# Weights of the last and the third pair from the end in column halves, other tile order and later residual reads at the end of a fused transformer and mixture-of-experts layer

## What is computed

```
x  = x + g1 * (concat([attn, rec]) @ w_out)          # "x1" below, the residual
h2 = modulate(rms_norm(x), sh2, sc2)
# top-1 of 4 groups, then top-2 of 8 experts inside it, weights in combine[n, e]
hg, hu = h2 @ w_gate[e], h2 @ w_up[e]                # 1024 -> 256
act    = silu(hg) * hu * combine[:, e]
y      = sum over e of act @ w_down[e]               # 256 -> 1024
out    = x + g2 * y
```

## Time and profile before

| what | us |
|---|---|
| median of 3 runs | 633.35 |
| the three runs | 629.74, 634.2, 633.35 |
| the profiled execution's own time | 631.55 |
| its span in the trace | 629.6 |

### The profile page before, as it was taken

How to read it: one execution, slowest core, us unless ns; L and a number is a source line. 1 busy time by engine, 2 the same in 40 slices (tenths; PEclk the granted TensorE clock), 3 DMA queues, 4 the chain that set the end, 5 groups by cost and what they waited for, 6 DMA issues and landing times.

```text
span 629.6 us, 9459 instructions
## 1 busy us (share of the span) xinstructions
PE 593.3 (94%) x3309; PEld 331.4 (53%) x3310; DVE 352.3 (56%) x788; ACT 177.5 (28%) x369; POOL 94.6 (15%) x131
## 2 busy tenths in 40 slices
PE   4989999999998999999999889999999999689797
PEld 2544555555565676645555445555555555355453
DVE  2736898765664888655666873343424334313337
ACT  4203887601144787731111101101110110011110
POOL 4000011122161000000000111212122121201200
PEclk9999999999999999999999999999999999989999
DMA  8999843330029629529114959999999999999876
GB/s 318 375 370 361 318 156 138 140 133 2 0 83 280 249 92 264 238 102 398 67 68 161 382 188 392 417 419 416 420 420 410 420 417 421 419 421 416 360 280 263
DMA packets 48273, 176.23 MB, mean 280 GB/s; under 512 B 10988, under 2 KB 18168, under 8 KB 34544
## 3 DMA queue, kind: packets, MB, share of 16 engines
q1 hardware_dynamic: 36992, 154.86, 63.0%
q0 software_dynamic: 6688, 15.58, 7.1%
q10 hardware_dynamic: 4560, 5.35, 2.4%
HBM read 163.31 MB, written 21.14 MB: 293 GB/s over the span
## 4 chain that ended last, share of the span: by engine, by line
PE 67%; DMA 15%; SPq 7%; DVE 6%; issue 2%; ACT 1%; ACTq 1%; POOL 1%; DVEq 0%; POOLq 0%
PE ps L1757 16%; PE ps L1574 11%; PE ps L1773 7%; PE ps L1490 7%; PE ps L1502 6%; DMA expert_w<-exp_w_up 5%; PE ps L1612 4%; PE ps L1639 4%; DMA gate_w<-lru_wx 3%; PE ps L1621 3%; DMA w_mod_ring<-w_mod 2%; SPq L329 2%; SPq L358 2%; PE ps L1465 2%; PE ps L1725 2%
## 5 line engine op out<-in xcount | busy, mean ns | idle before, releaser
L1757 PE MATMUL ps<-expert_w,hT_mixT 128*64 128x256 f32 x1120 | 137.1, 395 | 11.9 <-DMA expert_w<-exp_w_up 11.6
L1757 PEld LDWEIGHTS ps<-expert_w,hT_mixT 128*64 128x64 f32 x1120 | 84.8, 137 | 67.6 <-issue 23.0
L1490 PE MATMUL ps<-hT_mixT,w 128*128 128x128 f32 (+1 forms) x256 | 72.6, 437 | 1.2 <-DVE hT_mixT L918 1.2
L1574 PE MATMUL ps<-w,hT_mixT 128*128 128x512 f32 x160 | 71.9, 597 | 0.0
L1773 PE MATMUL ps<-expert_w,w 128*64 128x512 f32 x280 | 65.8, 598 | 0.0
L741 ACT ACTIVATE w<-ps 128x128 f32<-128x128 f32 x36 | 10.0, 278 | 194.4 <-PE ps L1757 194.4
L1304 DVE SCALAR_TENSOR_TENSOR w<-w,ps 128x128 f32<-128x128 f32 x36 | 10.4, 288 | 88.0 <-ACT w L741 88.0
L1490 PEld LDWEIGHTS ps<-hT_mixT,w 128*128 128x128 f32 x256 | 38.9, 191 | 35.8 <-issue 32.6
L1502 PE MATMUL ps<-w_qkv,hT_mixT 128*128 128x512 f32 (+1 forms) x160 | 53.2, 488 | 0.2 <-DVE v_tok L1006 0.2
L1322 DVE TENSOR_TENSOR w<-ps,w 128x1024 f32<-128x1024 f32 x17 | 20.8, 1225 | 56.5 <-PE ps L1773 56.5
L1574 PEld LDWEIGHTS ps<-w,hT_mixT 128*128 128x128 f32 x160 | 29.1, 191 | 29.9 <-issue 29.7
(11 more groups left out here) (289 smaller groups left out, 763.6 us busy)
## 6 DMA issues: line engine op xcount, KB each, us to landing
expert_w<-exp_w_down SPq DMA_DIRECT2D x31, 1024.0 KB, 18.5
expert_w<-exp_w_gate SPq DMA_DIRECT2D x29, 1024.0 KB
expert_w<-exp_w_up SPq DMA_DIRECT2D x29, 1024.0 KB
w_mod_ring<-w_mod SPq DMA_DIRECT2D x14, 1024.0 KB, 6.5
y_rows<-zero_rows POOLq DMA_DIRECT2D x10, 512.0 KB, 9.4
expert_w<-y_rows SPq DMA_DIRECT2D x10, 512.0 KB, 8.3
recurrence<-w_mod SPq DMA_DIRECT2D x8, 512.0 KB, 9.7
w<-w_in SPq DMA_DIRECT2D x4, 1024.0 KB, 16.9
```

The costliest lines, as they stand in the source:

```text
L1490: ins = pe.matmul(ps[:, bank, 0:n], w1v[:, c, m * P:(m + 1) * P], HM[:, c, lo:lo + n], start=(c == 0), stop=(c == DC - 1))
L1574: ins = pe.matmul(ps[:, 2 * (t % 2) + half, :], HM[:, c, t * P:(t + 1) * P], w1v[:, c, half * 512:(half + 1) * 512], start=(c == 0), stop= ...
L1757: ins = pe.matmul(ps[r, 2 + k, 0:2 * P].rearrange("p (k f) -> p k f", k=2), xT[:, c, r], gate_up(i)[:, :, c, k:FF:FC], start=(c == 0), sto ...
```

## The change

In `refill_for_halves` SP issues gate and up of pair 13 and of pair 15 as column halves: the four first halves, counted on a semaphore of their own (`lead_in` for pair 13, `halves_in` for pair 15), and then the four second halves, counted on `wgu_in[s]`. PE waits for the first halves ahead of the first half of its gate/up matmuls and for the second halves ahead of the second. The bytes are the same, and down is loaded as before. The x1b reads move behind the y_rows reads of the first two tiles, so behind the wait for the last scatter. The tiles at the end are worked in the order 3, 4, 0, 1, 2. Tiles 3 and 4 need no x1b, and no longer wait for it. PE_SUMS becomes 4, 0, 1. DVE does `with_second(3)` ahead of the last y's eviction.

```diff
-PE_SUMS = (1, 2, 3)
+ORDER = (3, 4, 0, 1, 2)
+PE_SUMS = (4, 0, 1)
...
+            def refill_for_halves(q, s, leading):
+
+                done = sp.value_load(last[0:1, q - HELD:q - HELD + 1])
+                sp.wait_ge(S["gu_mm"], done * FC)
+                for half in range(2):
+                    for j in range(2 * s, 2 * s + 2):
+                        for src, lo in ((wg_v, 0), (wu_v, EW)):
+                            sp.dma_start(ring[:, HOME[j], lo + half * EW // 2:lo + (half + 1) * EW // 2],
+                                         src[q * 2 + (j - 2 * s), :, half * EW // 2:(half + 1) * EW // 2])\
+                              .then_inc(wgu_in[s] if half else leading, 16)
+                sp.wait_ge(S["dn_mm"], done)
+                for j in range(2 * s, 2 * s + 2):
+                    w_down(sp, q * 2 + (j - 2 * s), j)
...
-            refill(PAIRS - 3, 1)
+            refill_for_halves(PAIRS - 3, 1, lead_in)
             refill(PAIRS - 2, 2, both=1)
             sp.dma_start(iota, ...)
-            refill(PAIRS - 1, 0)
-            sp.wait_ge(kept_in, 16 * 4)
-            for t in range(SPILLED):
-                sp.dma_start(x1b[:, t, :], a["x1_rows"][t * P:(t + 1) * P, :]).then_inc(kept_in, 16)
+            refill_for_halves(PAIRS - 1, 0, halves_in)
...
-            for t in range(NT):
+            sp.wait_ge(kept_in, 16 * 4)
+            for t in ORDER:
                 sp.dma_start(yk[:, t, :], ...).then_inc(rows_in[t], 16)
                 sp.dma_start(y0[:, t, :], ...).then_inc(y0_in[t], 16)
+                if t == ORDER[1]:
+                    for k in range(SPILLED):
+                        sp.dma_start(x1b[:, k, :], a["x1_rows"][k * P:(k + 1) * P, :]).then_inc(kept_in, 16)
...
             def with_second(t):
 
                 dve.wait_ge(rows_in[t], 32)
-                dve.wait_ge(kept_in, 16 * (4 + SPILLED))
+                if t < SPILLED:
+                    dve.wait_ge(kept_in, 16 * (4 + SPILLED))
...
+            with_second(3)
             last_y_evict(end)
+            with_first(3)
+            finish(0)
+            with_second(4)
             with_second(0)
-            with_first(0)
+            finish(1)
             with_second(1)
-            finish(0)
+            finish(2)
             with_second(2)
-            finish(1)
-            with_second(3)
-            with_second(4)
-            finish(2)
-            with_first(4)
+            with_first(2)
             finish(3)
             finish_last()
...
-                else:
+                elif not by_halves:
                     pe.wait_ge(wgu_in[s], visit * 64)
-                if s == 0 and not (isinstance(visit, int) and visit == 1):
+                if by_halves == 1:
+                    pe.wait_ge(lead_in, 64)
+                elif by_halves == 2:
+                    pe.wait_ge(halves_in, 128)
+                elif s == 0 and not (isinstance(visit, int) and visit == 1):
                     pe.wait_ge(halves_in, 64)
                 for half in range(2):
+                    if by_halves and half:
+                        pe.wait_ge(wgu_in[s], visit * 64)
```

More of the change, by code:

```diff
@@ L245, in build @@
         h2_at = [sem(f"h2_at{i}") for i in range(2)]
-        x1_at, last_rows, kept_in, halves_in = (sem(n) for n in ("x1_at", "last_rows", "kept_in", "halves_in"))
+        x1_at, last_rows, kept_in, halves_in, lead_in = (sem(n) for n in ("x1_at", "last_rows", "kept_in", "halves_in", "lead_in"))
         wm_in = [sem(f"wm_in{i}") for i in range(6)]
@@ L499, in _ @@
             sp.sem_inc(S["sp_turn"], 1)
-            for t in range(NT):
+            sp.wait_ge(kept_in, 16 * 4)
+            for t in ORDER:
                 sp.dma_start(yk[:, t, :], a["y_rows"][TOK + t * P:TOK + (t + 1) * P, :]).then_inc(rows_in[t], 16)
                 sp.dma_start(y0[:, t, :], a["y_rows"][t * P:(t + 1) * P, :]).then_inc(y0_in[t], 16)
-            for t in range(NT - 1):
-                sp.wait_ge(S["fin"], t + 1)
-                sp.dma_start(y_dst[t], yk[:, t, :]).then_inc(S["out_done"], 16)
+                if t == ORDER[1]:
+                    for k in range(SPILLED):
+                        sp.dma_start(x1b[:, k, :], a["x1_rows"][k * P:(k + 1) * P, :]).then_inc(kept_in, 16)
+            for i in range(NT - 1):
+                sp.wait_ge(S["fin"], i + 1)
+                sp.dma_start(y_dst[ORDER[i]], yk[:, ORDER[i], :]).then_inc(S["out_done"], 16)
             for half in range(2):
@@ L508, in _ @@
                 cols = slice(half * 512, (half + 1) * 512)
[L509 removed]
+                sp.dma_start(y_dst[ORDER[-1]][:, cols], yk[:, ORDER[-1], cols]).then_inc(S["out_done"], 16)
             sp.wait_ge(S["out_done"], 16 * (NT + 2))
@@ L1343, in with_first, with finish @@
                 step(dve.tensor_tensor(yk[:, t, :], yk[:, t, :], y0[:, t, :], ALU.add))
-            def finish(t):
-                dve.wait_ge(S["tail_mm"], t + 1)
-                b = 2 * t % 8
+            def finish(i):
+                dve.wait_ge(S["tail_mm"], i + 1)
+                t, b = ORDER[i], 2 * i % 8
                 dve.tensor_tensor(yk[:, t, :], yk[:, t, :], wide[:, b * 512:b * 512 + D], ALU.add)\
@@ L1351, in finish_last @@
             def finish_last():
-                b = 2 * (NT - 1) % 8
+                t, b = ORDER[-1], 2 * (NT - 1) % 8
                 for half in range(2):
@@ L1356, in finish_last @@
                     cols = slice(half * 512, (half + 1) * 512)
-                    dve.tensor_tensor(yk[:, NT - 1, cols], yk[:, NT - 1, cols], ps[:, b + half, :], ALU.add)\
+                    dve.tensor_tensor(yk[:, t, cols], yk[:, t, cols], ps[:, b + half, :], ALU.add)\
                        .then_inc(S["fin"], 1)
@@ L1730, in act_in, with step_of @@
                 pe.transpose(ps[:, 4 + 3 * c, 0:P], act2[:, c, :], ident[:, :]).then_inc(S["aT_mm"], 1)
-            def step_of(n, s, visit, kept=False):
+            def step_of(n, s, visit, kept=False, by_halves=0):
                 def gate_up(i):
@@ L1788, in _, with visits @@
             pe.wait_ge(S["route_ok"], 3)
-            def visits(q, s, visit, kept=False):
+            def visits(q, s, visit, kept=False, by_halves=0):
                 lo = pe.value_load(first[0:1, bass.ds(q, 1)])
@@ L1793, in visits @@
                 with pe.Fori(lo, hi) as n:
-                    step_of(n, s, visit, kept)
+                    step_of(n, s, visit, kept, by_halves)
             for s in range(HELD):
@@ L1800, in _ @@
             for q in range((BODIES - 1) * HELD, PAIRS):
-                visits(q, q % HELD, 1 + q // HELD, kept=q == KEPT // 2)
+                visits(q, q % HELD, 1 + q // HELD, kept=q == KEPT // 2, by_halves={PAIRS - 3: 1, PAIRS - 1: 2}.get(q, 0))
             steps = pe.value_load(last[0:1, PAIRS - 1:PAIRS])
@@ L1806, in _ @@
             pe.wait_ge(S["xT_a"], steps + 1)
-            for t in range(NT):
-                if t >= 4:
-                    pe.wait_ge(S["fin"], t - 3)
+            for i, t in enumerate(ORDER):
+                if i >= 4:
+                    pe.wait_ge(S["fin"], i - 3)
                 if t in PE_SUMS:
@@ L1812, in _ @@
                 for half in range(2):
-                    if t == 0:
+                    if i == 0:
                         pe.wait_ge(S["y_v"], steps + 1 + half)
                     if t in PE_SUMS:
-                        pe.matmul(ps[:, 2 * t % 8 + half, :], ident[:, :], y0[:, t, half * 512:(half + 1) * 512],
+                        pe.matmul(ps[:, 2 * i % 8 + half, :], ident[:, :], y0[:, t, half * 512:(half + 1) * 512],
                                   start=True, stop=False)
-                    ins = pe.matmul(ps[:, 2 * t % 8 + half, :], chosen[:, t, :],
+                    ins = pe.matmul(ps[:, 2 * i % 8 + half, :], chosen[:, t, :],
                                     y[:, half * 512:(half + 1) * 512], start=t not in PE_SUMS, stop=True)
-                    if half or t == NT - 1:
+                    if half or i == NT - 1:
                         ins.then_inc(S["tail_mm"], 1)
```

## The result

The change is slower, not faster: 634.34 us in the median of 20 runs against 632.32 for 20 runs of before, ratio 1.0036 with a 95% interval of 1.0023 to 1.0049, so 1.5 to 3.1 us and some 2.3. It lies inside my range and on the wrong side of no change. My rival 1 had this side and about this size (0.8 to 2.2 us), but not this path.

A forecast was written before the change was run, and what follows sets the result against it. It took the weight stream to bound late expert steps, and scatter plus reads the end. Pair 13's 0, pair 15's 4.8 us off the last path, and + 0.8 - 2.0 gave -1.2; it named 631.2 us, range 627.0 to 635.0.

The forecast's parts named there:

- rival 1: Tail bound by reads: x1b ahead of 603 delayed nobody; +0.8 us, with dear DMAs +2.2; chance 0.27.
- Pair 13: Its halves remove PE's 1.77 us wait, but PE then waits for pair 14's gate/up; gain taken as 0.
- Pair 15: Its halves let gate/up start at 593.0 without the 3.3 us wait; last step's path 4.8 us shorter.
- DVE's list: Tile 3's residual add moves into DVE's idle time before the eviction; 14.6 us behind it instead of 15.8.
- The reads: Tail reads start from 603.09 as before; three x1b reads among them make the last of 13 land at 623.4.
- + 0.8 - 2.0: Reads' path at the end: 0.8 us later by added x1b reads, 2.0 us earlier by x1b leaving the stream.
- Its path: The end hangs on the last of 13 reads, then 3.7 us of DVE and 3.3 us: 630.4.
- The pace: Tail reads land one after another at intervals of 1.34 us per 0.5 MB.
- The relief: x1b out of the stream ahead of 603 speeds the scatter and first reads; 0 to 3.8 us, taken as 2.0.
- -1.2: Predicted net change of the span, on the path through the tail's reads that ends last: 1.2 us faster.
- SP's queue: Eight more DMAs may hold SP longer, but its idle time from 580.5 to 603.09 covers it; no cost.
- Small DMAs: Halved weight DMAs cost 0.3 us, counted in the 2.0; by the fixed-cost rule some 14 us worse, thought unlikely.

The follow-up runs named there:

- dummies: The change with 12 dummy matmuls ahead of pair 14's step, filling PE's idle time there; ratio 1.0038 to before.
- pair 13 whole: The change with pair 13's weights loaded whole again instead of in halves; ratio 1.0036 to before.
- tail-alone trace: The change with all weights loaded whole as before, keeping its tile order and late x1b reads; ratio 1.0021 to before.
- the runs with dummies: The change with added dummy matmuls: 12 ahead of pair 14 (1.0038), or 6 (1.0053) or 3 (1.0027) where PE waits for tile 0's y0.
- 3 dummies: The change with 3 dummy matmuls of 512 columns where PE waits for tile 0's y0; ratio 1.0027 to before.
- early x1b: The change with the three x1b reads back in front of the wait for the last scatter; ratio 0.9989 to before.
- the run with all edits together: The change with pair 13 whole, x1b reads early, eviction before tile 3's add, and PE's matmuls needing no y0 first; ratio 0.9981 to before.

## Why the prediction was wrong, point by point

- **Pair 13: right.** 0 us, since pair 14's weights are late next. The new wait there was 1.2 to 2.4 us in the traces where I had 1.7, and both runs on it show no effect within their 0.2%. That the clock can fall in this wait I had not said; with dummies in it the time was the same.
- **Pair 15: right on its path.** 593.0 and 7.42 us, 0.3 us of waiting for down. By the steps' own measure 4.7 of the 4.8 us were there.
- **DVE's list: half right.** The add ahead of the eviction isn't hidden: it waits for tile 3's rows and holds the eviction back by 1.6 us in the trace with pair 13 whole (PE waits 0.2 to 3.1 us for the eviction in the other traces with pair 15 in halves and the add in front).
- **The reads: this is the step that failed**, the term "+ 0.8 - 2.0" of the sum, in three parts.
  - *Its path.* I let the end hang on the last of 13 reads and 3.7 us of DVE. The longer path starts at the ninth, tile 0's y0: 607.3 + 8 x 1.34 = 618.0 by my own numbers, then 3.4 us of PE, 6.1 us of five DVE operations and 3.3 us, 630.8 instead of 630.4.
  - *The pace.* In the tail-alone trace SP's first read went out at 602.5 and landed 3.7 us later, at 606.2, and tile 0's y0 landed at 618.8. That makes eight intervals of 1.58 us, not 1.34, 1.9 us more; 5.5 us of them lie between the landing of the first x1b read (612.0) and that of the next y_rows read (617.5), three intervals. Why these were slower no run shows. PE's sum took 3.7 us, 0.3 more.
  - *The relief.* I took 2.0 us for x1b leaving the stream, and the first read landed at 606.2 instead of 607.3, so 1.1 us.

  So 0.8 + 0.4 + 1.9 + 0.3 - 1.1 = 2.3 us where I had -1.2, and the tail-alone trace has 631.9 against 629.6. This account is of one traced execution; the timed runs of the tail alone put the loss at 1.3 us (0.3 to 2.3).

  Nor is the relief one number. With x1b late the scatters issued at 595.4 to 596.4 took 6.8 to 7.1 us to land, against 7.58 and 7.78 with x1b early; but the one issued at 597.6 took 5.3, against 7.3 for those issued at 597.2 with x1b early. There my 2.0 us came, and they are in the change's own trace too (599.48, 4.97 us). The path and the pace are what that could not pay for.
- **What I left out: PE's idle time turns into a lower clock where its work lies on the path.** Pair 15's halves bring PE to the tail 5 us sooner and x1b keeps tile 0's y0 away, so it idles 2.7 to 4.2 us in three traces, and the sum of tile 0 takes 5.4 us instead of 3.7. This fits with the tail alone (1.0021, idle 1.88 us, sum 3.7) being no slower than the change (1.0036), although its last step ends 4.6 us later than with pair 15 in halves and pair 13 whole (610.4 against 605.8). But the intervals of those two overlap, and the runs with dummies did not settle the share of the clock.
- **SP's queue: right.** SP took pair 15's down at 583.3 to 585.4 instead of 575.3, and was idle from there to the reads.
- **Small DMAs: right.** Halves alone, of either pair, changed nothing (1.0002, 0.9997). The Trainium skill, "DMA: Bandwidth & Descriptors", section Bandwidth, says to batch DMAs to 1 MiB or more. The loss of some 14 us, which the prediction works out from the fixed time of some 2 us that the same page gives to each DMA (section "Anatomy of one DMA — SWDGE (gpsimd) path", so for DMAs issued by GpSimd, where these come from SP), did not come.
- **Rivals.** Rival 1 came nearest: its +0.8 to +2.2 us lies against 2.3 measured (1.5 to 3.1), and its sign, a last read landed behind 623, was there (624.4 in the tail-alone trace). Its reason was not: it wanted a relief under 0.8 us, where the tail-alone trace has 1.1, and the last read isn't what the end waited for. That it had the size is in part luck. I gave it 0.27, and the evidence for its side was in my own text: 4.0 us added against 3.3 us of slack. I had bought the sign with a relief taken from the middle of 0 to 3.8 us. That the measured time lies inside my range says little, since the range held both signs.

## What to carry to other kernels

Before work is moved behind a wait, walk every consumer of the queue it joins, not the last one: the read with the most work behind it sets the end, here the ninth of 13. A gain on a path that doesn't end last isn't only worth nothing: an engine that arrives early may idle and start its next work at the lower clock, as PE did here. What can be done before a late operand arrives should stand ahead of the wait for it; that edit of a few lines gained 1.3 to 2.0 us in each of the three pairs of versions that differ by it.

## What the runs showed of the hardware

PE's clock fell after shorter idle times than I had counted with. In the run with all edits together, pair 13's gate/up came after 2.05 us of idle time and took 9.07 us instead of 7.47; with 1.77 us it had taken 7.47.

```profile
568.45 9.07 PE L1778 MATMUL ps<-expert_w,hT_mixT 128*64 128x256 f32 x64 [2.05 <-DMA expert_w<-exp_w_up]
```

Ahead of the 64 gate/up matmuls of pair 13 or 14 the traces have eight waits of 0.98 to 1.91 us with full clock behind them, and five of 2.05 to 2.43 us (2.05, 2.29, 2.30, 2.39, 2.43) with the lower clock and some 1.6 us more for the matmuls. So a wait for weights of some 2 us cost either 2 us or 3.6. And behind the same 3.31 us ahead of pair 15 the matmuls took 9.07 us in before's trace and 10.07 with pair 13's halves alone. The length of the wait alone doesn't decide it: in the tail, waits of 3.02 us (3 dummies) and 3.06 us (early x1b) for the eviction had the clock at 1.00 behind them, while 2.71 and 2.72 us for tile 0's y0 were followed by the lower one.

This may be part of why the kernel's runs spread by some 5 us whatever the variant. The two go together: of the 35 runs of before beside the first experiments, the 13 with a mean granted clock of 0.991 or more took 631.3 us on average, and the 10 with 0.985 or less 634.1. Which waits make the difference was not tested. How much of the change's loss beyond the tail alone is due to the clock stays open too.
